# Attention, merge, layer norm and selection in five token groups, woven with the gather steps of the group ahead

## What is computed

```python
def sparse_attention(aq, iq, iw, k_all, v_all, ik_all, limit):
    s = einsum('bqhd,bsd->bqhs', iq, ik_all) * (IDX_DIM ** -0.5)
    score = einsum('bqhs,bqh->bqs', relu(s), iw * (IDX_HEADS ** -0.5))   # 4 index heads
    sel_score, sel = lax.top_k(where(admissible, score, -inf), topk)     # 256 of up to 1024 keys
    ...                                                                  # 8 heads, softmax over the selected keys
def branch_merge(h, o_attn, o_gla, ...):
    m = sigmoid(gate_a) * (o_attn @ w_pa) + sigmoid(gate_b) * (o_b @ w_pb)   # gates = h @ w_in[:, C_GATE:]
    return m @ w_out
def peer(h, w_pq, pk1, pk2, pu, pv):      # h1 = layer_norm(alpha*x + branch_merge(...))
    q = (h @ w_pq).reshape(n, 8, 2, 128)                 # 16 query blocks of 128
    v1, i1 = lax.top_k(q[:, :, 0] . pk1, 16); v2, i2 = lax.top_k(q[:, :, 1] . pk2, 16)
    ...                                                  # 16 best of the 16 x 16 sums -> 128 experts e per token
    a = gelu(einsum('nhkd,nd->nhk', pu[e], h))           # 128 gathered rows of 1024 floats per token
    return einsum('nhk,nhkd->nd', g * a, pv[e])          # and 128 more; then layer norm 2
```

## Time and profile before

| | |
|---|---|
| median of 3 runs | 4807.19 us (4800.33 to 4821.35) |
| the profiled execution | 4851.24 us, of which the span of the trace is 4849.2 us |
| linear attention and projections, 0 to 705 us | 705 us |
| attention, 705 to 1303 us | 598 us |
| merge, 1303 to 1474 us | 171 us |
| output product and layer norm 1, 1474 to 1620 us | 146 us |
| queries of the first group and first selection, 1620 to 1716 us | 96 us |
| from the first to past the last indirect DMA, 1716 to 4849 us | 3133 us |

### The profile page before, as it was taken

How to read it: one execution, slowest core, us unless ns; L and a number is a source line. 1 busy time by engine, 2 the same in 40 slices (tenths; PEclk the granted TensorE clock), 3 DMA queues, 4 the chain that set the end, 5 groups by cost and what they waited for, 6 DMA issues and landing times.

```text
span 4849.2 us, 31290 instructions
## 1 busy us (share of the span) xinstructions
PE 2672.0 (55%) x10141; PEld 1164.9 (24%) x10141; DVE 2586.4 (53%) x5930; ACT 417.1 (9%) x780; POOL 2396.4 (49%) x2124
## 2 busy tenths in 40 slices
PE   9889898888999821542333334553333332333344
PEld 4444445555664610210000111120000000000000
DVE  0322328998213599665655566576555655554321
ACT  1110123333200100000000000000000000000000
POOL 0000000000000067777777777777777777777775
PEclk9778988897699955765555666775555555655556
DMA  2100100000110378999999999999999999999998
GB/s 83 34 1 2 52 22 14 14 13 1 63 42 26 93 255 303 364 388 350 381 379 366 370 352 370 378 356 350 370 383 364 383 383 371 373 370 356 337 366 296
DMA packets 405568, 1184.93 MB, mean 244 GB/s; under 512 B 39952, under 2 KB 125264, under 8 KB 405280
## 3 DMA queue, kind: packets, MB, share of 16 engines
q0 software_dynamic: 304384, 1107.96, 61.0%
q1 hardware_dynamic: 101024, 74.99, 5.1%
HBM read 1176.60 MB, written 6.20 MB: 244 GB/s over the span
## 4 chain that ended last, share of the span: by engine, by line
POOL 41%; issue 13%; DMA 4%; PE 4%; DVE 4%; ACT 0%; POOLq 0%; SPq 0%; DVEq 0%
POOL v_rows L1300 21%; POOL u_rows L1289 20%; DMA v_rows<-in_pv,expert_turned 4%; PE acc L1356 2%; PE side_ps L1321 2%; DVE u_rows L1574 2%; DVE key_at L1431 0%; DVE key_top L1428 0%; DMA w_pq_sb<-in_w_pq 0%; DMA u_rows<-in_pu,expert 0%; DVE key_scores L1435 0%; PE side_ps L1328 0%; DVE one_hot L1488 0%; DVE expert_f L1490 0%; DVE one_hot L1485 0%
## 5 line engine op out<-in xcount | busy, mean ns | idle before, releaser
L1289 POOL DMA_INDIRECT u_rows<-in_pu,expert x1056 | 1222.5, 1158 | 1559.2 <-DVE expert L1493 1191.0
L1356 PE MATMUL acc<-v_rows,weight_pad 128*32 128x512 f32 x4224 | 909.4, 1007 | 1731.1 <-DMA v_rows<-in_pv,expert_turned 1729.3
L1574 DVE CUSTOM_DVE_ANT_0 u_rows<-u_rows,late 128x1024 f32<-128x1024 f32 x1056 | 1269.6, 1225 | 1028.6 <-DMA u_rows<-in_pu,expert 1009.8
L1300 POOL DMA_INDIRECT v_rows<-in_pv,expert_turned x1056 | 1169.1, 1107 | 354.4 <-issue 312.3
L1356 PEld LDWEIGHTS acc<-v_rows,weight_pad 128*32 128x32 f32 x4224 | 174.8, 153 | 2410.7 <-issue 2404.7
L1321 PE MATMUL side_ps<-xT_sb,w_pq_sb 128*128 128x256 f32 (+2 forms) x768 | 257.9, 492 | 18.7 <-DMA w_pq_sb<-in_w_pq 9.5
L306 POOL DMA_DIRECT2D out_gla_p<-gla_S x4 | 2.4, 588 | 501.5 <-DVE gla_S L630 501.5
L930 DVE MAX8 m<-score 128x8 f32<-128x384 f32 (+6 forms) x209 | 183.4, 878 | 5.3
L1321 PEld LDWEIGHTS side_ps<-xT_sb,w_pq_sb 128*128 128x128 f32 x768 | 152.9, 205 | 138.4 <-issue 87.4
L932 DVE MATCH_REPLACE8 score<-m,score 128x384 f32<-128x384 f32 (+6 forms) x209 | 180.0, 861 | 0.0
L744 PE MATMUL att_pg<-xT_sb,w_b 128*128 128x352 f32 x384 | 157.5, 577 | 35.1 <-DVE mT L968 35.1
(11 more groups left out here) (196 smaller groups left out, 2900.2 us busy)
## 6 DMA issues: line engine op xcount, KB each, us to landing
w_pq_sb<-in_w_pq SPq DMA_DIRECT2D x48, 512.0 KB, 8.8
u_rows<-in_pu,expert POOLq DMA_INDIRECT x1056, 6.4
v_rows<-in_pv,expert_turned POOLq DMA_INDIRECT x1056, 6.4
xT_sb<-in_xT SPq DMA_DIRECT2D x8, 528.0 KB, 6.7
w_gvr<-in_w_in SPq DMA_DIRECT2D x2, 2048.0 KB, 13.1
w_gk<-in_w_in SPq DMA_DIRECT2D x8, 512.0 KB, 6.1
w_dsa<-in_w_in SPq DMA_DIRECT2D x2, 2048.0 KB, 10.3
w_b<-in_w_in SPq DMA_DIRECT2D x8, 512.0 KB, 4.1
```

The lines of the kernel that those rows point to most:

```text
L1289: pool.indirect_dma_start(out=U[:, n % RU, :], out_offset=None, in_=io["pu"], in_offset=bass.IndirectOffsetOnAxis(ap=expert[:, t % 2, k:k ...
L1300: pool.indirect_dma_start(out=V[:, slot, :], out_offset=None, in_=io["pv"], in_offset=bass.IndirectOffsetOnAxis(ap=turned[:, t % 2, at:at ...
L1356: last = pe.matmul(acc[32 * j:32 * (j + 1), t % 2, c * 512:(c + 1) * 512], pad[:, col:col + 32], V[:, (4 * n + y) % RV, c * 512:(c + 1) * ...
L1574: dve.tensor_tensor_reduce(U[:, n % RU, :], U[:, n % RU, :], h1[:, t, :], 1.0, 0.0, ALU.mult, ALU.add, dots[:, t % 2, k:k + 1]).then_inc(d ...
```

## The change

`gated_linear` stays, and `project_attention` also writes its turned queries (`aq_d`, `iq_d`) and the turned result of the linear branch (`ob_d`) to memory. All else becomes one function, `stream`, over five groups of tiles. A group's front is: load its queries and inputs, attention tile by tile, merge (16 steps of 12 products, each with its own 768 KB of weights), output, layer norm 1, the transposes of h1, 17 query steps, selection. `main(g)` is the gather part of a group. The program is the front of group 0, and then, for each group, its gathers woven with the front of the next group, by a cost for each step. The weights are loaded again for every group: `w_merge` 80 blocks instead of 16, `w_pq` 80 instead of 48, `w_out` five times instead of once. RU falls from 8 to 6, `acc` from two buffers to one, the v weights are padded in halves of 16, and four tiles of h1 are held instead of nine. In the attention the exponentials overwrite the logits, and `relu` and `score` have one buffer each instead of two.

```diff
+    FRONT = [[0], [1, 2], [3, 4], [5, 6], [7, 8]]
-    RU, RV = 8, 8
+    RU, RV = 6, 8
+    HS = 4
+    def attention_steps(t):
...
+        if chooses(t):
+            out += [("idx", t, h) for h in range(IH)]
+            out += [("round", t, r) for r in range(PARTS)]
+        out.append(("bias", t))
+        for i in range(HEADS + 2):
+            if i < HEADS:
+                out.append(("sc", t, i))
+            if i >= 2:
+                out.append(("va", t, i - 2))
+            if 1 <= i <= HEADS:
+                out += [("tu", t, i - 1, p) for p in halves(t)]
+        return out + [("fin", t)]
+    def front(g):
+        out = [("load", g)]
+        for t in FRONT[g]:
+            out += attention_steps(t)
+        out += [("mix", g, i) for i in range(2 * KD)]
+        out += [("out", t) for t in FRONT[g]] + [("h1t", t) for t in FRONT[g]]
+        out += [("query", g, b) for b in range(NB + 1)]
+        for t in FRONT[g]:
+            out += [("cand", t), ("best", t)] + [("pick", t, h) for h in range(PH)] + [("soft", t)]
+        return out
+    def main(g):
...
+            if t == 0:
+                out += us + [("weigh", 0)] + with_pads(vs) + [("norm", 0)]
+            elif t == 1:
+                out += us + [("weigh", 1)]
+            else:
+                out += woven(us, with_pads(gather(t - 1)[1])) + [("weigh", t), ("norm", t - 1)]
+        if g == NG - 1:
+            out += with_pads(gather(SAMPLE)[1]) + [("norm", SAMPLE)]
+        return out
+    program = list(front(0))
+    for g in range(NG):
+        program += woven(main(g), front(g + 1), 0.94) if g + 1 < NG else main(g)
+                def load_merge(n):
+                    g, i = divmod(n, 2 * KD)
+                    f, s = divmod(i, 2)
+                    if n >= 2:
+                        sp.wait_ge(mix_g, n - 1)
...
+                    sp.dma_start(wb[:, n % 2, 0:8, :], win[:, :, col:col + P]).then_inc(wb_in[n % 2], 16)
+                    sp.dma_start(wb[:, n % 2, 8:12, :], wp[:, :, f * P:(f + 1) * P]).then_inc(wb_in[n % 2], 16)
-        acc = ctx.enter_context(nc.psum_tensor("acc", [P, 2, D], F32))
+        acc = ctx.enter_context(nc.psum_tensor("acc", [P, D], F32))
```

More of the change, by code:

```diff
@@ L1183, in run_experts @@
-    fill, nth = {}, {}
-    for s in program():
-        if s[0] == "query":
+            return [[(j, x % HALF, 32 * j + x) for j in range(4)] for x in range(32)]
+        return [[(j, i, TS // 4 * j + i) for j in range(4)] for i in range(TS // 4)]
+    def attention_steps(t):
+        out = [("sample",)] if t == SAMPLE else []
+        if chooses(t):
[10 more added lines that the diff above has]
+        return out + [("fin", t)]
@@ new lines, in gather, with with_pads, woven @@
+    def gather(t):
+        us = [("u", t, k) for k in range(SLOTS[t])] if t < TILES else []
+        return us, [("v", t, i) for i in range(len(quads(t)))] if t < TILES else []
+    def with_pads(vs):
+        out = []
+        for s in vs:
+            if s[2] % HALF == 0:
+                out.append(("pad", s[1], s[2] // HALF))
+            out.append(s)
+        return out
+    def woven(one, two, upto=1.0):
+        at = []
+        for k, (x, end) in enumerate(((one, 1.0), (two, upto))):
+            total, run = sum(cost(s) for s in x) or 1.0, 0.0
+            for s in x:
+                at.append(((run + cost(s) / 2) / total * end, k, s))
+                run += cost(s)
+        return [s for _, _, s in sorted(at, key=lambda v: v[:2])]
@@ L1186, in run_experts @@
+    for g in range(NG):
+        program += woven(main(g), front(g + 1), 0.94) if g + 1 < NG else main(g)
+    slot, fill, kth, turn_at, u_at = {}, {}, {}, {}, {}
+    for s in program:
+        if s[0] in ("idx", "sc"):
+            slot[s] = len(slot)
+        if s[0] == "idx":
+            kth[s[1], s[2]] = len(kth)
+        elif s[0] == "tu":
+            turn_at[s[1:]] = len(turn_at)
+        elif s[0] == "query":
             if s[2] < NB:
@@ L1264, in _ @@
[L1264 to L1274 removed]
+                    sp.dma_start(wq[:, i % 2, :, :], wqv[:, :, b * P:(b + 1) * P]).then_inc(wq_in[i % 2], 16)
```

1171 lines of the change are left out of this document (570 added, 601 removed).

## The result

| | before | after |
|---|---|---|
| median, us (runs) | 4814.27 (4 runs, 4800.33 to 4829.96) | 4756.89 (4 runs, 4733.1 to 4765.33) |
| the profiled execution: time, span | 4851.24, 4849.2 | 4765.33, 4763.3 |
| first indirect DMA | 1715.9 | 892.6 |
| from the end of the first u step on DVE to the end of the span | 3128 | 3845 |

After stands to before as 0.9872, with a 95% interval of 0.9823 to 0.9921: 57 us faster, where 117 were forecast by the median. The sign is right, the time lies inside the range, and the gain is half of what I said.

What follows compares the result with a forecast made beforehand. Gathers at 1.43 us each were taken as the bound, or DVE where it has more to do: 954 us start + 3020 of gathers + 751 added by woven steps = 4725 of span, 4690 by the median; range 4450 to 4990.

Steps and rivals of the forecast that it cites:

- The start: Ahead of steady gathering: 705 us of linear branch and projections plus 249 for tile 0's front, 954 us.
- Key rounds and a group's loads: Key selection of tiles 2 to 8, set by DVE: 439 us of gathers plus 198 excess and 40 for loads, 677.
- The loads' own term: At a group's first score: its loads are waited for, 10 us net each, 40 us in all.
- Heads: Attention heads, bound by gathers: 522 us of gathers plus 37 of exposed work minus 72 of returned lead, 486.
- the credit for the lead: Attention heads: some 12 us of each gather lead built up in six key-round stretches come back, minus 72 us.
- Merge: Merge of groups 1 to 4: DMA is the slowest engine by little, 7.8 to 9.9 us a step, 573 us.
- The bytes' term: Merge: weights take 2.8 us of the DMA engines a step, beside gathers; 179 us over 394 of gathers.
- rival A: Merge and queries: weights land late, deciding from 13 us on; 427 us more in full, 4900 to 5110; chance 0.17.
- Output and queries: Output 112 us over its gathers, 228 in all; queries 120 over 407 of gathers, 527.
- B: Merge, queries and output: PE stays at its lower clock, 5030 us by the median; chance 0.10.
- C: Whole gather part: fronts disappear under the gathers as buffers level everything, 4240 us by the median; chance 0.10.
- D: Whole gather part: front and gathers wait for each other by turns, no overlap, no change in time; chance 0.08.

Runs made afterwards that it cites:

- e8: Changed kernel with every second pair of the key rounds left out, so half of the keys are chosen: 4614.8 us, ratio 0.9531 to the kernel before.
- e7: Changed kernel with a group's four loads ordered one selection earlier: 4727.23 us, ratio 0.9771 to the kernel before.
- e6: Changed kernel with four buffers for u rows instead of six: 4870.59 us, ratio 1.0064 to the kernel before.
- e4: Changed kernel with new weave cost numbers, moving gathers from attention heads into key rounds and outputs: 4722.8 us, ratio 0.9771 to the kernel before.
- e3: Changed kernel without weaving: all of a group's gathers first, then the next group's front: 5825.14 us, ratio 1.2047 to the kernel before.
- e5: Changed kernel with a third buffer for the query weights, ordered three steps ahead: 4722.59 us, ratio 0.9737 to the kernel before.
- e1: Changed kernel with a third buffer for the merge weights, ordered three steps ahead: 4706.83 us, ratio 0.9739 to the kernel before.
- e2: Changed kernel loading only the first two merge weight blocks in groups 1 to 4: 4591.17 us, ratio 0.9479 to the kernel before.
- e10: Changed kernel loading only the first two query weight blocks in groups 1 to 4: 4713.46 us, ratio 0.9758 to the kernel before.

## Why the prediction was half right

**What bounds the kernel.** Right. A gather costs 1.43 us, DVE limits where it has more to do, and both hold in after.

**The start.** Forecast 954, measured 918, with the first indirect DMA at 892.6 where 930 was said. Tile 0's merge took 83 us (106 in the sum, which had the loads of `w_out` ahead of it in full), queries 52 (62), output 16 (26 with layer norm and transposes). 36 us better.

**Key rounds and a group's loads.** Forecast 677, measured 657, and e8 shows that it is DVE. The loads' own term was too small: 10 us each was said, e7 took 42 away from three of them, at the end of the selection ahead and not in the rounds, where I had put it. So the rounds by themselves took 20 us more than the 637 of the sum.

**Heads: the first step that failed.** "Some 12 us of each lead come back in the attention heads behind, which are bound by gathers: minus 72." Heads took 602 us, not 486. Of these 116 us, 72 are the credit for the lead, which doesn't come back: counted between the cuts on DVE's timeline, POOL issued 374 gathers in the heads of tiles 1 to 8, where the order puts 365, and 294 in the key rounds, where it puts 308 (72 of 76 in tile 7's rounds). The key rounds build up no lead that the heads could spend, and e6 bears it out.

The other 44 us are waits: the heads took 80 us over their 522 of gathers, where 37 were said. That gathers bind them holds in the main, since e4 took 143 us of gathers out and they fell by 137. But on their own they take 10 us each at 1024 keys (e3), 459 us in all, so for most tiles the two lie near each other. Tile by tile the larger of the two adds up to 535 us; 602 is 67 more than that. Part of the waits stand at the ends: DVE waits 52 us in the eight stages for the first result of the next stage, and the index scores' share of that, 21 us, the sum had put at nothing. The longest is in tile 7, where 14.5 of 119 us go by until the sample tile's first index score, on DVE and on PE:

```profile
3505.48 0.49 DVE L1331 TENSOR_SCALAR shared_one<-shared_one,iw 32x544 f32<-32x544 f32 x1 [14.53 <-ACT shared_one L1178]
```

```profile
3502.78 2.10 PE L1042 MATMUL front_ps<-ikT,iq_group 64*32 64x512 f32 x8 [8.41 <-DMA V<-in_vc]
```

The sample tile's cached values go into the buffer `V`, which SP may fill only when tile 7 has used it. What is left of the 67 us I put down to engines that wait for each other in lists of fixed order, as in the timelines above; no run separates it. PE's clock has a small part at most: with the same 73 gathers, tile 7's heads took 115 us at 0.71 in e5, against 119 at 0.63:

```profile
3365.00:3480.00 115.00, 79.34 (x376) 37.90 (x376) 55.14 (x102) 20.69 (x39) 81.57 (x73) 0.71 0.94 347
```

**Merge: the second.** Forecast 573, measured 637. "So DMA is last, by little" took the maximum of PE, DMA bytes and gathers, and left out that a block is ordered only when the second one before it is used up. The bytes' term was good: with a third buffer the merge takes 575 us, as forecast, and the DMA engines are 0.97 busy in group 3 (e1); the landing came on top. The 176 us of e2 are not that term, since 62 of them are the landing's, and what is left, 461 us, is more than the 394 of gathers. It is rival A, with its formula, at about a fifth of its price in the merge: 64 us, where 864 - 573 were written. My reason against it, that gathers run dry and the landing shortens, holds in part: the 56 blocks took 11.7 us on average, where A's price has 21, but 23 of them took over 13, the prediction's own sign of A. I had made A a case with a chance of its own that starts at 13 us; it is a term that belongs in the sum from the first gather on, and it is in the queries too (41 us, e5).

**Output and queries.** 199 and 491 instead of 228 and 527: 65 us too much, which hid over a third of the 180 us of the two misses above. The queries' excess over 407 us of gathers was 84 and not 120 (106, if only the 269 gathers are counted that the order puts between the cuts on DVE's timeline), and 65 of it go when the weights aren't loaded (e10).

**Rivals B, C and D.** B's clock is wrong for merge and queries: 0.87 and 0.86 were granted in group 3, where the sum itself had 0.71 for the merge. C would need stages that level out; they don't. D falls with e3.

**The bookkeeping.** By stages: start -36, heads +116, key rounds and loads -20, merge +64, output -29, queries -36, rest -24: 35 of the 38 us between 4725 and 4763; the other 3 lie behind DVE's last instruction. That the span came so near is luck: 180 us too little in heads and merge stand against 145 too much in the other five. The other half of the miss by the median is the scaling: I took over that a profiled execution lies 0.9% above the median, 4725 to 4684. In after it lies 0.2% above (4765.33 against 4756.89), which is worth 35 us. That was a single pair of numbers, and its spread should have been in the range and not in the forecast. The range's lower end has a slip too: it takes "the 72" as a cost that may fall away, but in the sum it is a credit, and without it the forecast rises.

**What stays open.** Why leaving out 29 MB of query weights gives so little over a third buffer, when 44 MB of merge weights give 114 us. The heads' chain was read from timelines and fits e3, e4 and e6, but how much of the 67 us it is stays open; more than six u buffers, which would test it from the other side, were not tried.

## What to carry to other kernels

When two streams are woven in one order, work out each stage also alone, with its waits and not only the busy time of its engines; where the two come near each other, expect more than the larger (here 602 us of heads against 535). Look at the ends of stages as well, where an engine waits for the first result of the next. Buffers smoothed inside a stage here; they didn't carry work from a stage that is slow into one that is fast; so put the gathers where the other stream leaves their engines idle, by measured costs. And a load that is ordered n steps ahead sets a step of at least (landing + use) / n, with the landing beside the other traffic, not alone.

## What the runs showed of the hardware that was not expected

A merge block of two DMAs, which land in 4.1 and 4.4 us with little beside them, takes 4.6 to 24.3 us beside the gathers, 11.7 on average. The issue of its second DMA, 0.58 us at the median, took over 1 us in 27 of the 62 cases behind 1000 us and once kept SP's queue for 9.92 us:

```profile
2734.34 0.37 SPq L912 DMA_DIRECT2D w_merge<-in_w_in  x1
2734.75 9.92 SPq L913 DMA_DIRECT2D w_merge<-in_w_pa  x1
```

PE's clock can't be told from its busy share alone. In the heads of tile 7 alone (e3) PE was busy for 70 of 86 us and was granted 0.50; in the queries of group 3 of the same run, with 128-row products, it was busy for 58 of 66 and granted 0.98:

```profile
3878.00:3944.00 66.00, 58.49 (x284) 50.23 (x284) 45.09 (x255) 12.25 (x31) 0.00 (x0) 0.98 0.36 104
```

With v steps and 54 gathers beside them (e4) the same heads had 0.84. And DMA engines that are 0.96 busy aren't always the limit: in the queries of group 3 the share fell from 0.96 in after to 0.87 in e10, and the stage only from 129 to 115 us:

```profile
2910.00:3025.00 115.00, 85.04 (x428) 56.83 (x426) 87.80 (x329) 12.58 (x32) 75.74 (x69) 0.84 0.87 312
```
